# Decays of the state-space stage by one matmul per four heads, and a new order of convolution, silu and weight split on VectorE

## What is computed

```python
zxbcdt = h @ w_in                                  # z, x, B, C, dt
xbc = silu(causal_conv_of_4_taps(xbc) + conv_b)
# per block of 128 tokens, per group and head:
cs = cumsum(dt * A)
seg = cs[:, None] - cs[None, :]
decay = exp(where(causal, seg, -inf))
cb = einsum('bign,bjgn->bgij', C, B)
y_intra = einsum('bgij,bijgh,bjghp->bighp', cb, decay, x * dt)
```

## Time and profile before

| | us |
|---|---|
| median of 3 runs | 2491.5 |
| lowest and highest run | 2491.36, 2493.8 |
| the profiled execution | 2492.02 |
| its span, first to last instruction | 2490.2 |

### The profile page before, as it was taken

One profiled execution on the slowest core, in us unless ns is written; L12 is line 12 of the kernel. 1 busy time (PEld: TensorE's weight loads), 2 busy tenths in 40 slices (PEclk: granted clock), 3 DMA queues, 4 the chain that ended last, 5 costly groups with the idle time before them and its releaser, 6 DMA issues.

```text
span 2490.2 us, 33976 instructions
## 1 busy us (share of the span) xinstructions
PE 2445.7 (98%) x12490; PEld 2070.6 (83%) x12490; DVE 1600.6 (64%) x2144; ACT 1126.7 (45%) x1574; POOL 44.8 (2%) x75
## 2 busy tenths in 40 slices
PE   6999999999999999999999999999999999999998
PEld 5888888887888888888888888888888888888886
DVE  6777777776558656546556568555785565654655
ACT  4444444444436434434444454454553443443442
POOL 1000000000000000000000000000000000000000
PEclk8999999999999999999999999999999999999999
DMA  7555555544647656556566546235575655656653
GB/s 216 169 162 160 161 160 150 157 149 162 224 157 226 223 192 187 193 182 199 192 189 187 190 147 220 103 106 187 162 232 193 188 192 190 187 191 194 187 192 112
DMA packets 486487, 446.28 MB, mean 179 GB/s; under 512 B 13616, under 2 KB 359904, under 8 KB 485072
## 3 DMA queue, kind: packets, MB, share of 16 engines
q1 hardware_dynamic: 484608, 433.61, 55.9%
q0 software_dynamic: 1744, 10.81, 1.2%
HBM read 442.26 MB, written 2.10 MB: 178 GB/s over the span
## 4 chain that ended last, share of the span: by engine, by line
PE 91%; DVE 5%; ACT 2%; DMA 1%; issue 1%; POOL 0%; SPq 0%; DVEq 0%; ACTq 0%; POOLq 0%
PE ps L441 25%; PE ps L459 15%; PE ps L461 15%; PE ps L460 15%; PE ps L443 12%; DVE wlo L1251 2%; PE ps L512 2%; PE ps L596 1%; PE ps L493 1%; PE ps L491 1%; PE ps L492 1%; ACT whi L838 1%; PE ps L751 1%; PE ps L731 1%; DMA xin<-in_x 1%
## 5 line engine op out<-in xcount | busy, mean ns | idle before, releaser
L1251 DVE TENSOR_TENSOR wlo<-raw,whi 128x1024 fp32r<-128x1024 f32 x818 | 997.1, 1224 | 614.4 <-ACT whi L838 604.5
L838 ACT ACTIVATE whi<-raw 128x1024 fp32r<-128x1024 f32 x818 | 860.9, 1057 | 749.9 <-PE ps L461 484.7
L441 PE MATMUL ps<-actA,whi 128*128 128x512 f32 x2704 | 961.5, 400 | 6.5 <-DVE wlo L1251 5.2
L443 PE MATMUL ps<-actA,wlo 128*128 128x256 f32 x2704 | 758.1, 280 | 0.0
L441 PEld LDWEIGHTS ps<-actA,whi 128*128 128x128 f32 x2704 | 510.2, 189 | 131.0 <-issue 7.3
L443 PEld LDWEIGHTS ps<-actA,wlo 128*128 128x128 f32 x2704 | 512.5, 190 | 2.1 <-issue 1.7
L459 PE MATMUL ps<-whi,actB 128*128 128x512 f32 x1056 | 412.6, 391 | 0.0
L461 PE MATMUL ps<-whi,actB 128*128 128x512 f32 x1056 | 411.0, 389 | 0.0
L460 PE MATMUL ps<-wlo,actB 128*128 128x512 f32 x1056 | 410.9, 389 | 0.0
L461 PEld LDWEIGHTS ps<-whi,actB 128*128 128x128 f32 x1056 | 198.2, 188 | 41.4
L459 PEld LDWEIGHTS ps<-whi,actB 128*128 128x128 f32 x1056 | 198.3, 188 | 41.0
(11 more groups left out here) (220 smaller groups left out, 1813.0 us busy)
## 6 DMA issues: line engine op xcount, KB each, us to landing
raw<-in_mlp_w SPq DMA_DIRECT2D x512, 512.0 KB, 4.0
raw<-in_a_w_in SPq DMA_DIRECT2D x162, 512.0 KB, 4.0
raw<-in_a_w_out SPq DMA_DIRECT2D x64, 512.0 KB, 4.2
raw<-in_b_w_q SPq DMA_DIRECT2D x32, 512.0 KB, 4.5
raw<-in_b_w_o SPq DMA_DIRECT2D x32, 512.0 KB, 3.6
raw<-in_kv_w SPq DMA_DIRECT2D x16, 512.0 KB, 3.5
gb<-in_ln_g POOLq DMA_DIRECT2D x4, 1024.0 KB, 7.3
gb<-in_ln_b POOLq DMA_DIRECT2D x4, 1024.0 KB, 9.7
```

Source lines behind the costliest of these rows:

```text
L441: e.matmul(ps[:, b, :].rearrange("p (a n) -> p a n", a=2), whi[:, s, w], act[:, kt, :, :], start=(kt == 0), stop=False)
L443: last = e.matmul(ps[:, b, T:2 * T], wlo[:, s, w], act[:, kt, 0, :], start=False, stop=(kt == KT - 1))
L838: e.activation(whi[:, s, :], raw[:, r, :], ACT.Copy).then_inc(w_hi_done, C.up(w_hi_done))
L1251: e.tensor_tensor(wlo[:, s, :], raw[:, r, :], whi[:, s, :].bitcast(F32), ALU.subtract).then_inc(w_split, C.up(w_split))
```

## The change

- `seg` is one matmul of 512 columns for four heads. The stationary operand `css` holds cs (high and low part) and rows of ones, the moving one `csm` holds ones and minus cs, masked so that only the rows of the group's heads are not zero. The mask for causality is gone from PE.
- The transposes that feed it are 8 (into banks 6 and 7) and not 2; ACT copies both banks whole; DVE fills `csrc` with ones at the start and writes four small pieces where it wrote two.
- `csm` is written by POOL, `select(g, c)`, a multiplication of 128 x 1024 with two broadcast inputs, for each group and each block: 16 times where `sel8` was written 8 times. There is one buffer. POOL waits until PE has read it (`seg_read`, the semaphore of bank 6), and PE waits in `s3` too for `heads_selected`. POOL's loop is written out.
- ACT's `decay` takes -seg through Relu out of the two banks, then exp(-x) of 128 x 1024 in place. Above the diagonal that leaves exp(0) = 1, and the causal mask `tri` is multiplied into `bcb` instead, in `bc_out`, which DVE does where ACT had `a1`.
- ACT's `cross` writes straight into `xpad` and `conv` adds in place; the buffer `crossb` is gone.
- On DVE `conv(1)` to `conv(5)` each come one weight split earlier and ahead of the silu; after the last group `silu(5)` comes ahead of the split.

```diff
     def seg(c, hh, b):
         fill(b)
-        o = ps[:, b, :].rearrange("p (h n) -> p h n", h=4)
-        e.matmul(o, ident_r[:, :], smask_r[:, :].unsqueeze(1).broadcast_to([P, 4, P]), start=True, stop=False)
-        e.matmul(o, ncs2[:, c, :], sel8[:, 4 * hh:4 * hh + 4, :], start=False, stop=False)
-        for h in range(4):
-            last = e.matmul(ps[:, b, h * P:(h + 1) * P], sel8[:, 4 * hh + h, :], cs2[:, c, :],
-                            start=False, stop=(h == 3))
-        last.then_inc(full[b], C.up(full[b]))
+        e.matmul(ps[:, b, :].rearrange("p (h n) -> p h n", h=4), css[:, c, 0, :], csm[:, 4 * hh:4 * hh + 4, :],
+                 start=True, stop=True).then_inc(full[b], C.up(full[b]))
...
     def s3():
+        e.wait_ge(heads_selected, C.next(heads_selected))
         seg(1, 0, 7)
         seg(1, 1, 6)
...
     def cs_transposes():
-        transposes(6, [cshl[:, c, :, :].rearrange("p a n -> p (a n)") for c in range(NH)])
+        for k in range(2):
+            transposes(6 + k, [csrc[:, k, c, 4 * i:4 * i + 4, :, :].rearrange("p g a n -> p (g a n)")
+                               for c in range(NH) for i in range(2)])
...
-    def a1():
-        e.wait_ge(full[6], C.next(full[6]))
-        e.activation(bcb[:, :, :].rearrange("p a n -> p (a n)"), ps[:, 6, 0:3 * P], ACT.Copy).then_inc(
-            free[6], C.up(free[6]))
...
     def decay(c):
         for hh, b in ((0, 7), (1, 6)):
             e.wait_ge(full[b], C.next(full[b]))
-            e.activation(em[:, c, hh * BLK:(hh + 1) * BLK], ps[:, b, :], ACT.Exp).then_inc(free[b], C.up(free[b]))
+            e.activation(em[:, c, hh * BLK:(hh + 1) * BLK], ps[:, b, :], ACT.Relu, scale=-1.0).then_inc(
+                free[b], C.up(free[b]))
+        for b in (7, 6):
+            e.wait_ge(free[b], C.now(free[b]))
+        e.activation(em[:, c, :], em[:, c, :], ACT.Exp, scale=-1.0).then_inc(decayed, C.up(decayed))
...
+    def bc_out():
+        e.wait_ge(full[6], C.next(full[6]))
+        e.tensor_copy(bcb[:, 0, :], ps[:, 6, 0:P])
+        e.tensor_tensor(bcb[:, 1:3, :], ps[:, 6, P:3 * P].rearrange("p (c n) -> p c n", c=NH),
+                        tri[:, :].unsqueeze(1).broadcast_to([P, NH, P]), ALU.mult).then_inc(
+                            free[6], C.up(free[6]))
...
     g7 = NG - 1
+    silu(5, 1)
     step()
-    silu(5, 1)
-    split_y(0)
+    split_y(0, {1: bc_out})
     z_out()
...
-    def select(g):
-        e.tensor_copy(sel8[:, :, :], sel2[:, bass.ds(g * GH, GH)].unsqueeze(2)
-                                  .broadcast_to([P, GH, P])).then_inc(heads_selected, C.up(heads_selected))
+    def select(g, c):
+        i = g // 4
+        e.tensor_tensor(csm[:, :, :], csx[:, c, i, :].bitcast(F32).unsqueeze(1).broadcast_to([P, GH, P]),
+                        selg[:, (g % 4) * GH:(g % 4 + 1) * GH].unsqueeze(2).broadcast_to([P, GH, P]),
+                        ALU.mult).then_inc(heads_selected, C.up(heads_selected))
+
+    def seg_read(g, c):
+        e.wait_ge(full[6], 3 + 4 * g + 2 + c)
...
-    def turn(g):
-        e.wait_ge(m_ready, C.next(m_ready, 2))
-        select(g)
+    e.wait_ge(cs_turned, C.next(cs_turned))
+    select(0, 0)
+    for g in range(NG):
+        seg_read(g, 0)
+        select(g, 1)
+        if g + 1 < NG:
+            seg_read(g, 1)
+            if g == 3:
+                e.tensor_copy(css[:, :, 0, :], css[:, :, 1, :])
+            select(g + 1, 0)
         e.wait_ge(y_squared, C.next(y_squared, 2))
         group_rstd()
```

More of the change, by code:

```diff
@@ L269, in build @@
     csr = place("csr", [P, NH, NHD], F32R, y_at + 24 * 1024)
-    cshl = place("cshl", [P, NH, 2, NHD], F32, y_at + 25 * 1024)
+    csrc = place("csrc", [P, 2, NH, NG, 4, GH], F32, y_at + 25 * 1024)
     assert y_at + 16 * 1024 > y_at + 4 * (K_END + 5 * P + P + 2 * P + 3 * NHD + 12 * P)
@@ L293, in build @@
     qT = put("qT", [P, 4, T])
+    otok = put("otok", [P, BLK])
     ps = nc.alloc_psum_tensor("ps", [P, 8, BLK], F32)
@@ L870, in _ @@
                 split_weights()
-            C.n[full[6]] += 1
-            C.n[full[7]] += 1
+            for b in (6, 7):
+                C.n[full[b]] += 1
+                C.n[free[b]] += 1
             def constants_out():
@@ L1136, in mlp_slab @@
                     if i == 0:
[L1137 removed]
+                        mlp_cross(15)
                     if i == 1:
@@ L1497, in group @@
                 conv(0, par)
+                bc_out()
                 step()
@@ L1500, in group @@
                 step()
+                conv(1, par)
                 silu(0, par)
@@ L1503, in group @@
                 step()
-                conv(1, par)
-                step()
                 d23(0)
                 step()
+                conv(2, par)
                 silu(1, par)
-                conv(2, par)
                 step()
@@ L1512, in group @@
                 step()
+                conv(3, par)
                 silu(2, par)
-                conv(3, par)
                 step()
@@ L1517, in group @@
                 step()
+                conv(4, par)
                 silu(3, par)
-                conv(4, par)
                 step()
@@ L1522, in group @@
                 step()
+                conv(5, par)
                 silu(4, par)
-                conv(5, par)
-                for _ in range(5):
+                for _ in range(6):
                     step()
@@ L1536, in _, with split_y @@
                 group(2 * i + 3, 1)
-            def split_y(half):
+            def split_y(half, after={}):
                 act = act1 if half else actA
@@ L1543, in split_y @@
                        act[:, 4 * g:4 * g + 4, 0, :])
+                    if g in after:
+                        after[g]()
             def add_block(nb, stats=False, first=False):
```

82 lines of the change are left out of this document (45 added, 37 removed).

## The result

| | before | after |
|---|---|---|
| median, us | 2491.4 | 2466.3 |
| lowest and highest run | 2489.5, 2493.8 | 2464.16, 2467.14 |
| the profiled execution | 2492.02 | 2467.14 |
| its span | 2490.2 | 2465.3 |

The changed kernel takes 0.9895 of the time of before (95% interval 0.9881 to 0.9908, which is 22.9 to 29.6 us less); the medians differ by 25.1 us. The forecast was 21.9 us less, 2469.6 with a range from 2466.5 to 2476.5. The 3.2 us between are what the experiments had to find.

What follows compares the result with a forecast made beforehand. The prediction took PE's issue to bound the groups: 2492.0 - 21.9 (fewer matmuls) + 0.7 (transposes) + 0.3 (POOL) - 1.0 (after the last group) = 2470.1 us, median 0.5 lower, 2469.6, range 2466.5 to 2476.5.

Steps and rivals of the forecast that it cites:

- seg: PE in s2 and s3: three 0.23 us matmuls replace 2.06 us, 1.37 us gained a pair, 21.9 us for 16.
- rival 4: New seg matmuls on PE pay the slow pitch, 0.28 us each: 1.6 us less gain, 2471; chance within the forecast's 0.78.
- Transposes of cs: PE, once in the first group: eight transposes (1.09 us) for two (0.38 us), 0.7 us more.
- POOL: POOL's multiplication takes 2.4 us: no PE wait at s3 in seven groups, 0.3 us after the last.
- The margin for em: DVE ends d23(0) before PE takes em for block 0: margin 4.8 us before, 0.8 or more after.
- the CAST of 1.20 us: POOL's nearest row, read as having the memory to itself; doubled for two inputs to 2.4 us.
- ACT and bc_out: ACT's added exp, at most 2.1 us a group, and DVE's bc_out, 0.65 us, cost PE nothing.
- DVE's order: Earlier conv removes DVE's 1.43 us idles; earlier silu 5 ends PE's xT wait after the last group, 1.0 us gained.
- The step after the last group: PE's 2.84 us xT wait goes and split_y is late next: 1.0 us gained; 6.2 us less over the whole stretch.
- the forecast wait for actA: PE after the last group waits 1.5 to 2 us for actA in place of 2.84 for xT.
- The sum: Whole kernel: 2492.0 - 21.9 + 0.7 + 0.3 - 1.0 = 2470.1 us, median 0.5 lower, 2469.6 us.

Runs made afterwards that it cites:

- mask_new: Kernel before with each seg cut to one matmul, the mask alone, and DVE's new order, without the change's added work: 2465.9 us, ratio 0.9899.
- order_back: Changed kernel with DVE's old order (conv after the split and the silu, silu(5) behind the split after the last group): 2492.8 us, ratio 1.0003.
- mask_only: Kernel before, in DVE's old order, with each seg cut to the first of its six matmuls, the mask: 2475.8 us, ratio 0.9937.

## Why the prediction was right, and where it failed

**seg: right.** 1.37 us for a pair came out as 1.36 with nothing added (2.72 a group in mask_new) and 1.31 in the changed kernel. Sixteen of them are what carried the forecast; rival 4, the slow pitch, did not happen.

**Transposes of cs: right.** 0.7 forecast, 0.63 measured.

**POOL: right on the side, high on the size.** 1.90 us for 2.4, no wait at `s3`, none after the last group either, where 0.3 was put down. By the estimate from the table of the Trainium skill, "GPSIMD Engine Reference", section "Elementwise — side-by-side cycle accounting", it would have been 2.2. The contention was real as well. The rule of the Trainium skill, "SBUF — State Buffer", section "Who interferes with whom", that a two-input DVE instruction stands still while POOL holds the ports, agrees with 2.92 us for `d23(0)` against 1.22. The 1.67 us pass has one input in SBUF. The same section names such a `tensor_scalar` too, where it runs in a mode that uses both ports. Whether it did, no trace here shows: undisturbed it took 0.41 us, about as long as a two-input pass of that size (0.42). The margin for em was given as 0.8 us or more and is 2.8. One row was misread: the CAST of 1.20 us did not have the memory to itself, for a convolution pass of DVE ran beside it and took 0.68 us where 0.41 is usual.

**ACT and bc_out: right for the changed kernel, but not for the reason given.** They were called free because ACT is busy for half of the group and `bc_out` ends three us before bank 6 is needed. In the old order the same work cost up to 20 us over six groups (405.2 against 385.3). They are nearly free, 0.1 us a group, because the convolutions come earlier. The forecast had not looked at this, so that it held here is partly luck.

**DVE's order: the step that failed in its reasoning.** The prediction valued it at the 1.0 us after the last group and used it otherwise only to say that DVE's idles go. It redid DVE's order to em, and did not look at the banks that `conv` frees, nor at ACT, which waits behind each `conv`. Without the order the change is worth nothing (order_back, 2492.8). A shorter PE alone it does not need: mask_only, in the old order, gains 14.7 us in the six groups where mask_new gains 16.3. The order is what makes room for the added work. Since the change held both halves, this didn't move the sum.

**The step after the last group: right.** 6.4 us for 6.2 in that stretch, and the forecast wait for actA, 1.5 to 2, is 2.15. The second execution of each kernel gives 4.4 for the same stretch (75.11 - 70.70), with a granted clock of 0.70 in the changed one, so the close agreement is partly luck.

**The sum: the step that failed in size.** It went over the instructions that the diff edits and took all others to cost the same. One didn't: new operands moved act1 by 1920 bytes, and 2.05 us came from there, two thirds of the miss of 3.2. The step that failed is this term, put at nothing without a look at the addresses. In the table the rest is the start, 1.5 us, against which the groups gave 0.6 less than forecast. The scatter of the start is as large as that, so the cause of this part stays open. The stretches that repeat (groups, transposes, output projection, and the step within its scatter) give 21.6 to 23.6 us of the 25.1. With the layout's 2.05 us the forecast would have been 24.0 us less, inside the measured interval, so no more of the miss than this one term is clear of the noise. That the median fell 0.2 us outside the range and not inside is chance. The range was built from rivals that all cost time; a larger gain than forecast had only 2 chances in 100, and the range's low end had no bound from it.

## What to carry to other kernels

When PE is made shorter, look for the circle through the other engines that was hidden just behind it: follow from each engine's longest wait who is queued behind the waiting instruction, and compare the length of that circle with PE's new time. Test a change of two halves by each half alone, since two halves that are worth nothing apart can be worth 25 us together. If an edit adds or drops a buffer, list which operands of the later stages move, and allow for their pace.

## What the runs showed of the hardware

- A stream of 512-column matmuls ran at 0.232 us each with its moving operand in a buffer that starts at a multiple of 1024 bytes, and at 0.227 where it starts 896 bytes beyond one, at the same granted clock, set and unset by a pad. In the same traces the column blocks that read actA or actB ran at 0.227 too; these start 128 bytes beyond such a multiple. Other offsets weren't tried, nor which access it is that meets there.
- A DVE pass with one input in SBUF (TENSOR_SCALAR, 128x256, 0.41 us) took 1.67 us beside a POOL multiplication of 1.90 us.
- After PE had stood for 5.3 us (mask_only), its granted clock was 0.63 in the window of 5 us in which the wait ended and 0.69 in the next; after 2.15 us it stayed at 1.00 in one execution of the changed kernel and was 0.70 in another.
